# Two hybrid blocks in one kernel: own SBUF places for each feed-forward stage's first two panels, and rebuilt layer norms

## The reference

```python
def hybrid_layer(x, ...):                     # first block, twice, then rmsnorm
    h = rmsnorm(x, g_mix); z = h @ w_in
    ...                                       # window attention, chunkwise retention
    mixed = sigmoid(ga) * ya + sigmoid(gb) * yb
    x = x + mixed @ w_out
    h2 = rmsnorm(x, g_mlp)
    return x + square(relu(h2 @ w_up)) @ w_down

def second_block(x, ...):                     # twice
    y = hybrid_mixer(x, ...)                  # indexer attention, gated linear attention
    x = layer_norm(DN_ALPHA * x + y, ln1_g, ln1_b)
    y = conv_ffn(x, ...)                      # up, 3-tap conv, gelu(a) * b, down
    x = layer_norm(DN_ALPHA * x + y, ln2_g, ln2_b)

def layer_norm(x, g, b):
    mu = mean(x); var = mean(square(x - mu))
    return (x - mu) * rsqrt(var + LN_EPS) * g + b
```

## Time and profile before

| | |
|---|---|
| median of 3 runs | 3583.14 us (3582.88 to 3584.63) |
| the profiled execution | 3583.21 us, its span 3581.4 us |
| PE busy | 3433.8 us, 96% |
| DVE, ACT, POOL busy | 44%, 40%, 40% |
| mean granted PE clock | 0.986 |
| DMA | 83 GB/s mean |

### The profile page before, as it was taken

The page is one execution under the profiler, slowest core; times in us unless marked ns, Lnnn a source line. Parts: engine busy times, 40 slices in busy tenths (PEclk is TensorE's granted clock), DMA queues, the critical chain, the costliest instruction groups (busy, mean ns, idle before and its releaser), DMA issues.

```text
span 3581.4 us, 45406 instructions
## 1 busy us (share of the span) xinstructions
PE 3433.8 (96%) x16314; PEld 2787.5 (78%) x16314; DVE 1581.5 (44%) x2407; ACT 1432.7 (40%) x2116; POOL 1438.9 (40%) x1100
## 2 busy tenths in 40 slices
PE   8999999999999999999999999999999999999997
PEld 6788878887688878887768886787777688867785
DVE  5624232226623432227862444434478514344435
ACT  4734232224734332223462444333344634353333
POOL 4334444444334444444323343444343233434442
PEclk9999999999999999999999999999999999999999
DMA  3122222222122322222202121222212121212221
GB/s 142 60 82 73 102 85 94 94 95 95 68 74 85 104 83 94 94 97 82 83 36 80 64 96 71 94 94 94 82 72 71 49 74 67 102 63 95 93 94 59
DMA packets 43811, 298.48 MB, mean 83 GB/s; under 512 B 4816, under 2 KB 5456, under 8 KB 8592
## 3 DMA queue, kind: packets, MB, share of 16 engines
q1 hardware_dynamic: 41696, 291.52, 22.9%
q10 hardware_dynamic: 1968, 4.94, 0.4%
HBM read 294.34 MB, written 2.10 MB: 83 GB/s over the span
## 4 chain that ended last, share of the span: by engine, by line
issue 54%; POOL 32%; PE 11%; DVE 1%; ACT 1%; POOLq 1%; DVEq 0%; ACTq 0%
POOL w_lo L310 32%; PE ps L432 4%; PE ps L433 3%; PE ps L434 3%; PE ps L516 0%; POOLq L305 0%; DVE arena L1672 0%; ACT arena L1125 0%; POOLq L309 0%; DVE x L1708 0%; DVE arena L1696 0%; DVE tmp L1496 0%; ACT y_hi L1144 0%; DVE x L1945 0%; ACT x L1459 0%
## 5 line engine op out<-in xcount | busy, mean ns | idle before, releaser
L310 POOL TENSOR_TENSOR w_lo<-w_raw,w_hi 128x512 fp32r<-128x512 f32 x1096 | 1438.7, 1344 | 2100.1 <-ACT w_hi L947 2100.0
L432 PE MATMUL ps<-x_hi,w_hi 128*128 128x512 f32 x2752 | 1099.7, 400 | 29.3 <-DVE x_lo L1481 15.6
L433 PE MATMUL ps<-x_lo,w_hi 128*128 128x512 f32 x2752 | 1077.5, 392 | 0.0
L434 PE MATMUL ps<-x_hi,w_lo 128*128 128x512 f32 x2752 | 1077.4, 392 | 0.0
L947 ACT ACTIVATE w_hi<-w_raw 128x1024 fp32r<-128x1024 f32 x548 | 547.6, 1048 | 490.2 <-PE ps L434 490.2
L432 PEld LDWEIGHTS ps<-x_hi,w_hi 128*128 128x128 f32 x2752 | 520.5, 189 | 177.8 <-issue 40.6
L434 PEld LDWEIGHTS ps<-x_hi,w_lo 128*128 128x128 f32 x2752 | 519.9, 189 | 111.1
L433 PEld LDWEIGHTS ps<-x_lo,w_hi 128*128 128x128 f32 x2752 | 520.8, 189 | 106.9 <-issue 2.9
L432 PE MATMUL ps<-y_hi,w_hi 128*128 128x512 f32 x1248 | 489.6, 392 | 17.8 <-DVE x L1708 13.0
L433 PE MATMUL ps<-y_lo,w_hi 128*128 128x512 f32 x1248 | 486.5, 390 | 0.0
L434 PE MATMUL ps<-y_hi,w_lo 128*128 128x512 f32 x1248 | 486.2, 390 | 0.0
(11 more groups left out here) (187 smaller groups left out, 3121.6 us busy)
## 6 DMA issues: line engine op xcount, KB each, us to landing
w_raw<-stream SPq DMA_DIRECT2D x274, 1024.0 KB, 4.8
x<-x_t SPq DMA_DIRECT2D x4, 512.0 KB, 5.7
rotary<-rot ACTq DMA_DIRECT2D x4, 512.0 KB, 3.6
y_t<-x SPq DMA_DIRECT2D x8, 256.0 KB, 2.1
ct<-consts ACTq DMA_DIRECT2D x2, 770.0 KB, 5.2
arena<-pos ACTq DMA_DIRECT2D x2, 256.0 KB, 3.4
vec<-vectors ACTq DMA_DIRECT2D x4, 116.0 KB, 2.0
ct<-consts ACTq DMA_DIRECT2D x1, 128.0 KB, 4.1
```

Of the source, the lines that this page charges most:

```text
L310: ins = nc.gpsimd.tensor_tensor(WL[:, s, c:c + S], RAW[:, s, c:c + S], WH[:, s, c:c + S].bitcast(F32), ALU.subtract)
L432: pe.matmul(ps, wh, xh, start=(k == 0), stop=False)
L433: pe.matmul(ps, wh, xl, start=False, stop=False)
L434: return pe.matmul(ps, wl, xh, start=False, stop=last)
```

## The change

Four things are done together.

1. **Own places.** Panels `ff` and `ff + 1` of each of the four feed-forward stages get own buffers for their high and low parts (`OWN_H`, `OWN_L`), laid over the upper 16 units of the arena. ACT converts both among the `wo` panels (`hi_own`), waiting for the arena to be free and no longer for PE to leave a slot. `ff + 2` is then converted where `ff + 1` was in the first block, and behind tile 3 of ln1's loop in the second; its place inside `up(0)` is gone. POOL's loop is cut into stretches between the own panels.
2. **Layer norms.** The squares go to eight buffers (`YSCR`), without a wait for PE. `warm_root` stands ahead of the squares. The gain and bias are applied twice from the same input (first to `XH`, then in place to `X`), without ACT's waits for itself.
3. **Dummies.** PE runs 6 dummy matmuls ahead of the mean and 2 between the mean and the squares, all in bank 6; the 10 behind the sums stay.
4. **Four tiles side by side.** In the second block PE's first group is `first_up`: for k = 0 to 5 all four tiles, then tile by tile k = 6, 7.

```diff
+        own_place = {at(l)["ff"] + p: p for at in (at_a, at_b) for l in range(DEPTH) for p in range(2)}
+        def high(c):
+            return OWN_H[own_place[c]] if c in own_place else WH[:, c % 2, :]
...
+            first = 0
+            for end in sorted(c for c, p in own_place.items() if p == 0) + [NPANELS]:
+                with pool.Fori(0, (end - first) // 2) as i:
+                    low_half(first, i, 0)
+                    low_half(first, i, 1)
+                for c in range(end - (end - first) % 2, min(end + 2, NPANELS)):
+                    low_half(c, 0, 0)
+                first = end + 2
...
+                def first_up():
+                    pe.wait_ge(up_read, base_t)
+                    for p in range(2):
+                        pe.wait_ge(lo_ready, ff + p + 3)
+                    steps = [(k, j) for k in range(KD - 2) for j in range(4)]
+                    steps += [(k, j) for j in range(4) for k in (KD - 2, KD - 1)]
...
-                up(0, 0)
+                if kt == 2:
+                    first_up()
+                else:
+                    up(0, 0)
...
+                    keep_clock(6, 3)
                     column_sums(lambda k: TMP[:, 2, :], 1, 4, ...)
-                    column_sums(lambda k: TMP[:, k % 2, :], KD, 5, ...)
+                    keep_clock(6, 1)
+                    column_sums(lambda k: YSCR[:, k, :], KD, 5, ...)
-                        keep_clock(4, 5)
+                        keep_clock(6, 5)
...
+            def hi_own(t, l, c):
+                rot = next_rot(l, t)
+                A.after((t, l, "merged_lo", 7), (t, l, "r_lo", 7), None if rot is None else ("b", rot, "rot_tables"))
+                hi(c)
...
-                for p in range(4):
+                for p in range(3):
                     hi(w["wo"] + p + 1)
...
+                hi_own(t, l, w["ff"])
+                run(squared, 2)
+                hi_own(t, l, w["ff"] + 1)
...
-                        elif gi == 0 and gc == 0:
-                            hi_up(1, 0, 0, 0)
-                        else:
+                        elif not (gi == 0 and gc == 0):
                             hi_down(gc - 1, gi, i, 0)
...
+                run(squared)
                 for k in range(4):
                     stream_hi(k)
-                hi(w["ff"] + 1)
+                hi(w["ff"] + 2, used=panel_used(w["wo"] + 2))
...
+                    warm_root()
-                    for _ in squares(..., lambda k: TMP[:, k % 2, :], ...,
-                            lambda k: (t, l, which + "_ms", k - 2) if k >= 2 else None, ...):
+                    for _ in squares(..., lambda k: YSCR[:, k, :], ..., lambda k: None, ...):
                         pass
-                    warm_root()
                     root(PS[:, 5, :], D, LN_EPS, ...)
-                    if which == "ln1" or l + 1 < DEPTH:
-                        hi(w["ff"] + 1 if which == "ln1" else at_b(l + 1)["iq"] + 1)
+                    if which == "ln2" and l + 1 < DEPTH:
+                        hi(at_b(l + 1)["iq"] + 1)
                     for k in range(KD):
-                        A.after((t, l, which + "_scaled", k))
+                        A.after((t, l, which + "_scaled", k), own=False)
+                        if which == "ln1" or l + 1 < DEPTH:
+                            A.done(act.activation(XH[:, k, :], X[:, k, :], ACT.Identity, ...), ...)
                         A.done(act.activation(X[:, k, :], X[:, k, :], ACT.Identity, ...), ...)
-                        if which == "ln1":
-                            split_hi(XH[:, k, :], X[:, k, :], [], (t, l, "ln1_hi", k))
+                        if (which, k) == ("ln1", 3):
+                            hi(w["ff"] + 2, used=panel_used(w["wo"] + 2))
```

More of the change, by code:

```diff
@@ L942, in hi, with panel_used @@
                     act.wait_ge(*used)
[L943 to L947 removed]
+                elif c >= 2 and c not in own_place:
+                    act.wait_ge(*panel_used(c - 2))
+                wh = WH[:, s, :] if k else high(c)
+                for o in range(0, PANEL, 2 * S):
+                    act.activation(wh[:, o:o + 2 * S], RAW[:, s, o:o + 2 * S], ACT.Copy).then_inc(hi_ready, 1)
+            def panel_used(c):
+                who, n = marks.get(("panel", c), ("pe", 1))
+                return sems[who], n
+            def hi_own(t, l, c):
+                rot = next_rot(l, t)
+                A.after((t, l, "merged_lo", 7), (t, l, "r_lo", 7), None if rot is None else ("b", rot, "rot_tables"))
+                hi(c)
             def read(name, dst, func=ACT.Copy, *after, **kw):
```

77 lines of the change are left out of this document (44 added, 33 removed).

## The result

The changed kernel took 3556.83 us in the median of four runs (3554.40 to 3558.54), the kernel before 3583.31 us beside it (3582.88 to 3584.63): a ratio of 0.9924, with a 95% interval of 0.9912 to 0.9937. That is 26.5 us less; 27.7 had been forecast, and 3555.5 us. The profiled execution took 3554.40 us with a span of 3552.5, where before it was 3583.21 and 3581.4: the span lost 28.9 us.

What follows compares the result with a forecast made beforehand. PE bounds the kernel, busy 3433.8 of 3581.4 us; its idle and low-clock time can be won. Terms 14.9 + 7.4 + 1.9 + 3.5 = 27.7 us off 3583.21 gave 3555.5 us, range 3549 to 3564.

Steps and rivals of the forecast that it cites:

- First block, third panel: First block's feed-forward stages: PE's waits for `ff + 2` and the low clock behind them go, 14.9 us won.
- ln1, twice: Second block's ln1, both layers: last `wo` matmul to first product falls to 19.4 us, 8.2 us won.
- with the table loaded ahead it follows at once: At the norms: loading the table ahead removes the root's 0.51 us delay behind the sums.
- What ln1 gives back: Second block's feed-forward: PE waits 0.9 to 2.6 us for the fourth panel; 0.8 and 0 us taken off.
- the rival in which the wait grows to 4 or 5 us: Fourth panel comes 2 to 3 us later than reckoned, clock falls behind it: 9 us lost, 3564; chance 0.16.
- The ACT conversion in the midst isn't felt by PE: Second block's first group: four tiles need a new k each 2.7 us, ACT and DVE give one each 1.5.
- ln2: First layer's ln2: 1.4 us won in the norm, 0.5 by the clock behind it; 1.9 us in all.
- The last norm: Program's end: root 2.4 us sooner, at +13.1, and eight activations faster; 3.5 us won.
- the first block keeps its wait: Rival: `ff + 3` comes late in place of `ff + 2` in both layers, 3565; chance 0.10.
- the loops fall out of step: Rival: second block's 22 groups each get their panel 1.6 us late, 35 us lost, 3590; chance 0.04.
- the clock holds through the norms: Rival: clock stays 1.00 behind ln1 and ln2; ln2 gives 2.2 us more, ln1 nothing; 3550; chance 0.10.

Runs made afterwards that it cites:

- e2: Changed kernel with the first block's third-panel conversion (`ff + 2`) put back into its loop's first group: 3571.35 us, ratio 0.9967.
- e8: Changed kernel with the root's table load moved back behind the squares, eight square buffers kept: 3561.65 us, ratio 0.9933.
- e3: Changed kernel without the 6 and 2 dummy matmuls ahead of the sums in all four norms: 3563.71 us, ratio 0.9947.
- e6: Changed kernel with the second block's fourth panel (`ff + 3`) converted early, in the first group ahead of tile 2: 3552.67 us, ratio 0.9908.
- e9: Changed kernel with the third panel's conversion at the second block's ln1 moved from behind tile 3 to ahead of the root: 3560.91 us, ratio 0.9933.
- e7: Changed kernel with the second block's fourth panel converted early and two tiles side by side instead of four: 3563.88 us, ratio 0.9944.
- e5: Changed kernel with two tiles side by side instead of four in the second block's first group: 3563.46 us, ratio 0.9941.
- e10: e6's kernel; at ln2 and the last norm the first dummies don't wait for DVE's last addition, next panel's conversion ahead of the root: 3547.80 us.
- e11: e10's kernel with 16 instead of 10 dummy matmuls behind the sums: 3545.71 us, ratio 0.9896.
- e1: The control: the changed kernel measured again with no edit, beside the experiments: 3560.37 us, ratio 0.9934.
- e4: Changed kernel with the squares back in two alternating buffers, each waiting for the sum two before: 3563.38 us, ratio 0.9941.
- e12: Changed kernel with ln1's third-panel conversion ahead of the root and two tiles side by side instead of four: 3551.97 us, ratio 0.9919.

## Why the prediction was right, and where it was off

**First block, third panel** (14.9 us forecast): 15.2 by the stages. The waits and half of the low clock behind them were 9.85 + 5.1 us, so it is all the mechanism named. That edit taken back alone (e2) brings back 12.4 us: both waits whole, but 0.9 us less by the clock in the first layer, and 1.0 us a layer less since no conversion stands between the activations then. `ff + 3`, which had 2.3 us to spare by the forecast, was in time in both layers.

**ln1, twice** (8.2 us forecast): 4.7 + 3.5 = 8.2, and the stretch is the 19.4 us forecast. The parts hold as well: the sums 7.11 us (7.05 forecast; sixteen times the 0.43 us that it names are 6.9, and the last pass ends later than the next would start), the root to the first activation 4.90 us (4.91). One step inside was credited to the wrong cause: "with the table loaded ahead it follows at once". It follows at once with the load behind the squares too (e8), because eight buffers let the squares be done in time. The size was right, but the edit that was named for it is worth nothing beside the other one.

**What ln1 gives back** (0.8 and 0 us forecast): 2.4 and 1.7 us. This is the term that was mis-sized. The chain to the fourth panel was right, its parts to 0.3 us and its sum to a tenth: ACT came to the first two tiles 21.49 us behind its first activation (21.2 forecast), POOL's low part began 11.14 us later (11.4), PE started the panel 35.36 us behind the first matmul (35.3). The low part, of two panels in one go, in the timeline of POOL, and the panel in that of PE:

```profile
2217.12 9.95 POOL L338 TENSOR_TENSOR w_lo<-w_raw,w_hi 128x512 fp32r<-128x512 f32 x8 [19.67 <-ACT w_hi L994]
```

```profile
2222.25 0.49 PE L457 MATMUL ps<-x_hi,w_hi 128*128 128x512 f32 x1 [2.46 <-POOL w_lo L338]
```

What failed is the clock. The forecast had 1.7 us lost right behind the norm "as behind the first layer's norm", which would have made PE wait less. At ln1 it was held in both layers, so PE waited 2.46 and 2.45 us, inside the 0.9 to 2.6 given, and the clock fell behind that wait: 3.4 us at 0.50, 1.7 us lost, in each layer. That loss had been reckoned only for the rival in which the wait grows to 4 or 5 us. It is its mechanism at about a third of its price (3.3 us of 9). In e3 the clock did fall where the forecast had it, right behind the norm: the wait was 1.43 us, no stretch of 0.50 followed it, and the stages took 1.3 and 0.7 us more than before instead of 2.4 and 1.7. That the changed kernel had the other course was not in the forecast, and nothing here shows what decides between them. e6 and e9 show the price from both sides: without the wait the stage is up to 4.9 us shorter, and with a wait of 1.42 us there is no stretch of 0.50.

"The ACT conversion in the midst isn't felt by PE" was right, though at nothing the four tiles were undersold: with two, and the fourth panel early, that conversion costs 3.2 us of waits and the clock behind them (e7). In the changed kernel they are worth 0.1 and 2.1 us (e5), for they bring a wait of their own.

**ln2** (1.9 us forecast): 1.4 us in the stretch, as forecast (21.58 us against 21.5), and behind it 3.4 us at 0.50 instead of 6.8 before, of which 5.45 were work: 1.0 us, against 0.5 forecast. Sum 2.4. The 1.0 is in part luck: in six of the nine other traces whose ln2 keeps its dummies (e3, e10 and e11 change them) the stretch behind it was 6.8 us.

**The last norm** (3.5 us forecast): 3.8, of which 0.16 is the late start of the window in the earlier trace rows; the root at 13.18 us (13.1), the eight activations in 5.75 us (5.6 by the pace of two, half a microsecond more allowed for the stores):

```profile
3544.29 5.75 ACT L1520 ACTIVATE x<-x,vec 128x512 f32<-128x512 f32 x8 [4.21 <-DVE x L2004]
```

**The sum.** The terms as measured are 15.2 + 8.2 - 4.1 + 2.4 + 3.8 = 25.5 us; the spans differ by 28.9. The other 3.4 us lie in the mixers, where the change moves nothing but the own conversions, and where this execution has some 10 us less of 0.50 than the one before. That this is chance is an inference from the spread: the second layer's mixer took 554.0 us before, and 551.5 to 557.3 in the traces with the change. The difference of the medians was 26.5 us in the first measurement and 24.0 in the control (3584.33 and 3560.37), so the terms lie between the two. So the forecast of 27.7 was too high by the give-back of ln1 (3.3 us), and less for small gains at ln2 and the end; but a difference of a few microseconds is below what the medians can tell, and that 3556.83 lies so near to 3555.5 is in part luck: the control's median is 4.9 us above the forecast.

**The rivals.** That the first block keeps its wait and that the loops fall out of step did not happen. That the clock holds through the norms happened by half: it held behind ln1 in both layers and fell behind ln2. This rival had the consequence at ln1 right, a longer wait for the fourth panel, but put it at nothing, where it cost 3.3 us. Behind the fourth panel no group of the 22 waits for POOL: besides the two of 2.5 us there are four waits of 0.5 us, near 393, 1189, 2102 and 3068 us, ahead of the feed-forward stages, and they stood there before.

**Left open.** What e3 and e4 lose apart comes to 2.1 us in ln1's sums (1.53 and 0.53), which got 3.15 us shorter in the first layer. Both together weren't taken away; before, the sums spent 6.80 us at 0.50 there, and without the dummies only 3.4.

## What to carry to other kernels

Price a wait of a tuned matmul loop twice, by its length and by the clock behind it, and price the waits that a faster stage will meet next in the same way: here a norm won 4.7 us, and gave back 2.4 at the next panel. A place of its own for a panel is worth what it lets the converting engine do earlier, so look for the first conversion in its queue that moves; and fill idle time of the helping engine ahead of a wait (the root) rather than in the loop that feeds PE. Where the clock differs from run to run, compare the lengths of single stages between traces, and let medians decide only what is larger than their own scatter.

## What the runs showed of the hardware

- **A wait of 2.5 us cost the clock each time, one of 1.4 us never.** In the four traces in which PE waited 2.45 to 2.49 us for the fourth panel in both layers (the changed kernel, e1, e2, e4), the granted clock was at 0.50 for 3.4 us within 1.1 us of its end, eight times in eight. In the three with waits of 1.42 or 1.43 us there (e3, e8, e9), it stayed at 1.00 six times in six. In between lie the waits for `x_lo` in the first panel: behind those of 1.87 to 1.90 us (e5's second layer, e7's both) it fell three times in three, for 6.8 us, behind one of 1.71 us (e5 at 2203.64) it did not. Length alone doesn't decide: behind the 3.01 us of idle time at the end of ln1 it stayed in some traces (the changed kernel, both layers) and fell in others (e6 at 2191.7, e12 at 3152.5) with the same instructions ahead. Of the 22 times that ln1 ran with the dummies of the change (two layers, eleven kernels) it fell in 6. What tells these apart was not tried.
- **The scatter.** The kernel before ran at a mean granted clock of 0.986, the changed one at 0.990 to 0.994 from run to run, and its times spread over 7.6 us in five runs where those of before, taken beside them, spread over 3.3 in ten.
- **DVE beside POOL.** The same scaling takes 0.68 us alone and 1.78 while POOL makes a low part (2191.34 to 2197.45); the subtraction takes 0.69 us alone, and 0.94 and 1.78 in that time:

```profile
2190.96 0.69 DVE L2004 TENSOR_TENSOR x<-x,tmp 128x512 f32<-128x512 f32 x1
...
2193.66 0.94 DVE L1540 TENSOR_TENSOR x_lo<-x,x_hi 128x512 fp32r<-128x512 f32 x1 [2.02 <-ACT x L1520]
2194.52 1.78 DVE L2004 TENSOR_TENSOR x<-x,tmp 128x512 f32<-128x512 f32 x1
2196.22 1.78 DVE L1540 TENSOR_TENSOR x_lo<-x,x_hi 128x512 fp32r<-128x512 f32 x1
2197.92 0.68 DVE L2004 TENSOR_TENSOR x<-x,tmp 128x512 f32<-128x512 f32 x1
```

  The reciprocal, with one input, took 3.35 us at ln2 with POOL at work beside it, as it did at ln1 without. The Trainium skill ("SBUF — State Buffer", the section on SBUF's two separate sides) has it so: outside DVE's two-port modes, the lock between the two engines concerns DVE instructions with two SBUF inputs, against GpSimd instructions that read SBUF, and the trace agrees.
